# Eighteen feed-forward up pairs of a decoder layer in Strassen's form, with the down projection as a phase of its own

## The chip, the core and the metric

The kernel runs on one core of a Trainium2 chip (trn2). The metric is device time in microseconds, the median of several executions; one further execution is taken by the hardware profiler, and all rows below are from it. The engines are TensorE (PE, with its weight loads as PEld), VectorE (DVE), ScalarE (ACT), GpSimd (POOL) and the queue engine SyncE (SP), which issues most of the DMAs.

## The reference, cut to what matters

One decoder layer for 1,024 prompt tokens and 8 x 4 sample tokens, T = 1,056 tokens in all, in float32. The change lies in the last third of the layer, the feed-forward:

```
h2 = rmsnorm(x, w['norm2_g'])
up = h2 @ w['ffn_up']                      # 1024 -> 2 * 2816
up_ext = concatenate([ffn_hist, up])       # 2 tokens of history
g_ff, u_ff = split(causal_dwconv(up_ext, w['ffn_conv_w'], w['ffn_conv_b']))   # 3 taps
x = x + (silu(g_ff) * u_ff) @ w['ffn_down']                                   # 2816 -> 1024
```

A final RMSNorm follows, and the last two rows of `up_ext` are an output too.

## The kernel before

Data lie channels first: 128 channels on the partitions, the 1,056 tokens along the free axis, cut into three chunks of 352 columns (CH). A product in nearly full float32 precision is made of three matmuls in the fp32r format: each operand is split into an upper part (cast to fp32r) and a lower part (the remainder), and hi x hi, hi x lo and lo x hi are summed in PSUM. `product` (line 1968) does one block of 128 output channels so: 8 k-blocks x 3 parts x 3 chunks = 72 matmuls of 352 columns, each with its own weight load. The input projections, the gates, the output projection and the up projection all use it.

The feed-forward works on 22 pairs of blocks, a gate block and an up block of 128 channels each. Per block: SP loads 128 weight columns (512 KB) into a ring of three buffers, GpSimd casts and subtracts (`split`, lines 884 to 888), TensorE runs `product` into ps0 or ps1 (three PSUM banks each), DVE evicts with the norm factor (`ffn_tokens`), ACT does the first tap of the convolution (line 1345), DVE the other two (line 1894), ACT the silu (1348), DVE the product (1900), ACT and DVE split the result into act_hi and act_lo (1355, 1906). The down projection of each two pairs (24 sets of 6 matmuls of 352 columns, `down`, lines 2518 to 2541) stands in TensorE's program between two up blocks of later pairs; its sets alternate between the two banks pt0 and pt1, and DVE adds each into the residual x1 = y_all in SBUF (`ffn_sums`, line 1914). A loop turn on every engine is two pairs. The order of the instructions is written out by hand, engine by engine, with semaphores. A helper, `Order.run`, makes an engine wait for its own last result before it goes on.

Ahead of it stands the output projection (`out_block`), whose result is x1; `second_norm_upper` and `second_norm_lower` make h = x1 * norm gain in two parts, and the row factor rstd (a square root on ACT, a reciprocal on DVE) is applied at eviction. At the end, TensorE turns the history rows (`turn_ffn_state`, 44 transposes) and the result (`turn_tile`), ACT and DVE normalize, and SP stores. `TAIL` and `TAIL_DVE` give the order of the last sums and tiles.

Of the kernel before, what the change touches and what calls it, by code (L numbers as in the profile page):

```python
# [29 lines left out]
P = 128  # L30
# [18 lines left out]
FH = 2  # L49
EPS = 1e-6  # L50
# [69 lines left out]
class Order:  # L120
# [31 lines left out]
    def enter(self, i, first, extra=()):  # L152


        per = {name: n - self.before.get(name, 0) for name, n in self.n.items()}
# [11 lines left out]
def decoder_layer(nc, a, o):  # L167
# [15 lines left out]
    h_hi = sb(top, "h_hi", [P, KD, T], F32R)  # L183
    h_lo = sb(top, "h_lo", [P, KD, T], F32R)
    y_all = sb(top, "y_all", [P, 2 * 4, T])
    w_raw = [sb(top, f"w_raw{n}", [P, KD, P]) for n in range(2)]
    w_hi = [sb(top, f"w_hi{n}", [P, KD, P], F32R) for n in range(2)]
    w_lo = [sb(top, f"w_lo{n}", [P, KD, P], F32R) for n in range(2)]
# [158 lines left out]
    ld_pw, ld_ws = sem("ld_pw"), sem("ld_ws")  # L347
# [4 lines left out]
    w_zeroed, small_zeroed, a_zeroed = sem("w_zeroed"), sem("small_zeroed"), sem("a_zeroed")  # L352
# [9 lines left out]
    dk_abs, dk_exp, dk_u, dk_ln = sem("dk_abs"), sem("dk_exp"), sem("dk_u"), sem("dk_ln")  # L362
    alog_exp, sdt_done = sem("alog_exp"), sem("sdt_done")
    a_sum, a_rms, va_done, u_done = sem("a_sum"), sem("a_rms"), sem("va_done"), sem("u_done")
    wst_done, wsm_done, pd_done = sem("wst_done"), sem("wsm_done"), sem("pd_done")
    pstate_in, pstate_out, y_a_done = sem("pstate_in"), sem("pstate_out"), sem("y_a_done")
# [30 lines left out]
    def ptf_of(b):  # L397
# [52 lines left out]
    att_zeroed, att_rows, v_done = sem("att_zeroed"), sem("att_rows"), sem("v_done")  # L450
# [3 lines left out]
    c_zeroed, sx_ready, clog_in, clog_done = sem("c_zeroed"), sem("sx_ready"), sem("clog_in"), sem("clog_done")  # L454
    ld_pages, ld_lf, ld_v = sem("ld_pages"), sem("ld_lf"), sem("ld_v")
    ld_k = [sem(f"ld_k{n}") for n in range(2)]
    ss_max, ss_exp, ss_done = sem("ss_max"), sem("ss_exp"), sem("ss_done")
    x_conv, x_act, xstate_in, xst_ready, z_done = (sem(n) for n in ("x_conv", "x_act", "xstate_in", "xst_ready",
                                                                    "z_done"))
    d_zeroed, ld_d, eacs_done = sem("d_zeroed"), sem("ld_d"), sem("eacs_done")  # L460
# [5 lines left out]
    d_rms, yd_ready = sem("d_rms"), sem("yd_ready")  # L466
# [14 lines left out]
    s46 = ExitStack()  # L481
    hist_f = sb(s46, "hist_f", [9 * FH, 2 * FF])
    fh = sb(s46, "fh", [P, 2 * NFF, NB * FH])
    fstate = sb(s46, "fstate", [P, 2 * NFF, 9 * FH])
    f_raw = w_raw + [sb(s46, "w_raw2", [P, KD, P])]
    f_hi = w_hi + [sb(s46, "w_hi2", [P, KD, P], F32R)]
    f_lo = w_lo + [sb(s46, "w_lo2", [P, KD, P], F32R)]
# [5 lines left out]
    ones_m = sb(s4, "ones_m", [P, P])  # L493
    s4.close()
    ext = [sb(s46, f"ext{n}", [P, FE_W + 4]) for n in range(2)]
    cv = [sb(s46, f"cv{n}", [P, FE_W]) for n in range(2)]
    act_hi = sb(s46, "act_hi", [P, 2, T], F32R)
    act_lo = sb(s46, "act_lo", [P, 2, T], F32R)
    s46.close()

    y_out = [f_raw[n][:, :, :].rearrange("p k n -> p (k n)") for n in range(3)]
    gfin = ext[1][:, 0:D]
# [11 lines left out]
    ones_done, nm_full, nm_rms, h2_hi_done, h2_split = (sem(n) for n in ("ones_done", "nm_full", "nm_rms",  # L514
# [2105 lines left out]
```

## Time and profile before

| | |
|---|---|
| runs | 1920.19, 1922.92 and 1929.63 us, median 1922.92 |
| the profiled execution | 1923.46 us, of which the trace spans 1921.7 us |
| mean granted TensorE clock | 0.986 |
| TensorE busy | 96% of the span, 11,458 matmuls |
| VectorE, GpSimd, ScalarE busy | 47%, 30%, 21% |
| DMA | 113.51 MB, mean 59 GB/s |

The feed-forward lasts from about 1114 us to the end. Matmuls overlap in the trace: a matmul's recorded duration is longer than the distance to the next one's start, and rates are read from the starts.

### The profile page before, as it was taken

How to read it: one execution, taken by the hardware profiler on the slowest of the kernel's cores; microseconds unless marked ns; L12 is line 12 of the kernel's file. 1: busy time of each engine (PE TensorE's matmuls, PEld its weight loads, DVE VectorE, ACT ScalarE, POOL GpSimd, SP SyncE). 2: the span in 40 equal slices, each digit the busy share in tenths (PEclk: the TensorE clock that was granted, in tenths of full speed). 3: DMA queues.
4: the chain of work that ended last, by engine and by line, in shares of the span. 5: the costliest groups of instructions: out<-in, count | busy, mean ns of one | idle time of the engine just before them, and what ended most of it. 6: DMA issues, size and time to landing. Idle time of an engine off the chain costs nothing.

```text
span 1921.7 us, 29631 instructions
## 1 busy us (share of the span) xinstructions
PE 1849.8 (96%) x11458; PEld 1776.4 (92%) x11458; DVE 908.9 (47%) x1390; ACT 404.2 (21%) x583; POOL 582.9 (30%) x532
## 2 busy tenths in 40 slices
PE   5899999999999998999999999999999999999997
PEld 4889978888899978999999999999999999999986
DVE  5763244326533434222253375555555555555555
ACT  5210033423311112110121131111111111211123
POOL 2223310022233323334342324423432432432420
PEclk9899999999999989999999999999999999999998
DMA  4121130022122222232224311111111111211102
GB/s 126 46 53 38 46 90 23 12 83 67 39 86 68 69 73 73 62 94 72 68 77 108 100 34 55 45 35 54 55 33 44 55 44 33 64 45 33 55 11 99
DMA packets 156104, 113.51 MB, mean 59 GB/s; under 512 B 10743, under 2 KB 146652, under 8 KB 155991
## 3 DMA queue, kind: packets, MB, share of 16 engines
q1 hardware_dynamic: 153084, 102.61, 19.1%
q10 hardware_dynamic: 2940, 9.81, 1.3%
q8 instruction: 55, 0.90, 0.2%
q14 instruction: 25, 0.20, 0.0%
HBM read 95.37 MB, written 16.99 MB: 58 GB/s over the span
## 4 chain that ended last, share of the span: by engine, by line
PE 90%; DVE 5%; ACT 2%; DMA 1%; issue 1%; POOL 0%; ACTq 0%; SPq 0%; DVEq 0%; POOLq 0%
PE ps L1976 21%; PE ps L1982 20%; PE ps L1979 20%; PE ps L2413 5%; PE pt L2538 4%; PE pt L2540 4%; PE pt L2539 4%; PE ps L2185 2%; PE ps L2146 2%; PE pt L2171 1%; PE ps L2538 1%; PE ps L2540 1%; PE ps L2539 0%; PE ps L2118 0%; PE ps L2292 0%
## 5 line engine op out<-in xcount | busy, mean ns | idle before, releaser
L1976 PE MATMUL ps<-h_hi,w_hi 128*128 128x352 f32 x2472 | 549.6, 331 | 10.4 <-POOL w_lo L888 4.5
L1982 PE MATMUL ps<-h_hi,w_lo 128*128 128x352 f32 x2472 | 534.9, 324 | 0.0
L1979 PE MATMUL ps<-h_lo,w_hi 128*128 128x352 f32 x2472 | 534.5, 324 | 0.0
L1976 PEld LDWEIGHTS ps<-h_hi,w_hi 128*128 128x128 f32 x2472 | 417.5, 190 | 22.0 <-issue 13.6
L1982 PEld LDWEIGHTS ps<-h_hi,w_lo 128*128 128x128 f32 x2472 | 425.2, 189 | 0.0
L1979 PEld LDWEIGHTS ps<-h_lo,w_hi 128*128 128x128 f32 x2472 | 422.8, 189 | 0.0
L881 POOL TENSOR_TENSOR mark<-eps 128x1 f32<-128x1 f32 x159 | 52.2, 329 | 1080.4 <-PE ps L1982 558.0
L888 POOL TENSOR_TENSOR w_lo<-w_raw,w_hi 128x1024 fp32r<-128x1024 f32 x127 | 332.9, 2621 | 10.2
L1914 DVE TENSOR_TENSOR y_all<-y_all,pt 128x352 f32<-128x352 f32 x234 | 122.0, 522 | 104.7 <-PE pt L2540 104.5
L2538 PE MATMUL pt<-act_hi,w_hi 128*128 128x352 f32 x468 | 152.9, 327 | 3.7 <-DVE y_all L1914 2.2
L2540 PE MATMUL pt<-act_hi,w_lo 128*128 128x352 f32 x468 | 152.4, 326 | 0.0
L2539 PE MATMUL pt<-act_lo,w_hi 128*128 128x352 f32 x468 | 152.0, 325 | 0.0
L1894 DVE SCALAR_TENSOR_TENSOR cv<-ext,pv,cv 128x1072 f32<-128x1072 f32 x88 | 144.7, 1645 | 11.9 <-DVE cv L1894 0.2
L887 POOL CAST w_hi<-w_raw 128x1024 fp32r<-128x1024 f32 x127 | 133.0, 1047 | 0.0
L1345 ACT ACTIVATE cv<-ext,pv 128x1072 f32<-128x1072 f32 x44 | 56.6, 1287 | 305.0 <-DVE ext L1883 305.0
L1880 DVE TENSOR_TENSOR ext<-ps,cst 128x704 f32<-128x704 f32 x44 | 39.3, 893 | 123.4 <-PE ps L1982 123.0
L2538 PEld LDWEIGHTS pt<-act_hi,w_hi 128*128 128x128 f32 x468 | 88.9, 190 | 4.9 <-DVE y_all L1914 2.9
L1355 ACT ACTIVATE act_hi<-cv 128x1024 fp32r<-128x1024 f32 (+1 forms) x44 | 28.4, 646 | 302.7 <-DVE cv L1900 302.0
L2539 PEld LDWEIGHTS pt<-act_lo,w_hi 128*128 128x128 f32 x468 | 89.0, 190 | 0.0
L2540 PEld LDWEIGHTS pt<-act_hi,w_lo 128*128 128x128 f32 x468 | 88.8, 190 | 0.0
L1269 ACT ACTIVATE sg<-ps 128x1056 f32<-128x1056 f32 x16 | 16.9, 1053 | 214.2 <-PE ps L1982 214.2
L1809 DVE TENSOR_TENSOR sg<-sg,ps 128x1056 f32<-128x1056 f32 x8 | 10.0, 1254 | 85.8 <-PE ps L2413 85.7
(346 smaller groups left out, 1882.1 us busy)
## 6 DMA issues: line engine op xcount, KB each, us to landing
w_raw<-in_w_in SPq DMA_DIRECT2D x52, 512.0 KB, 4.4
w_raw<-in_ffn_up SPq DMA_DIRECT2D x44, 512.0 KB, 3.8
w_raw<-in_ffn_down SPq DMA_DIRECT2D x22, 512.0 KB, 3.5
gates_dram<-y_all ACTq DMA_DIRECT2D x16, 528.0 KB, 2.7
cst<-gates_dram SPq DMA_DIRECT2D x16, 528.0 KB, 3.6
x_tok<-in_x_prompt SPq DMA_DIRECT2D x8, 512.0 KB, 4.1
bw_raw<-in_w_branch SPq DMA_DIRECT2D x32, 128.0 KB, 3.5
w_raw<-in_w_out SPq DMA_DIRECT2D x8, 512.0 KB, 5.1
```

What stands on the lines that cost most here:

```text
L887: od.run(g.tensor_copy(hi, raw))
L888: od.run(g.tensor_tensor(lo, raw, hi.bitcast(F32), ALU.subtract), w_split)
L1345: od.run(sc.activation(cv[k][:, 0:FE_W - FH], x[:, 0:FE_W - FH], ACT.Identity, scale=param(PV_FW, blk), bias=param(PV_FB, blk)), cv0_done)
L1894: od.run(v.scalar_tensor_tensor(cv[k][:, 0:w], x[:, j:j + w], pv[:, bass.ds(blk + (PV_FW + 2 * NFF * j), 1)], cv[k][:, 0:w], ALU.mult, ALU ...
L1914: od.run(v.tensor_tensor(dst, dst, spare_or_pt(n, spare), ALU.add), dn_done)
L1976: mm(dst[:, c, 0:CH], f_hi[n][:, k, :], h_hi[:, k, tok], start=k == 0, stop=False)
L1979: mm(dst[:, c, 0:CH], f_hi[n][:, k, :], h_lo[:, k, tok], start=False, stop=False)
L1982: last = mm(dst[:, c, 0:CH], f_lo[n][:, k, :], h_hi[:, k, tok], start=False, stop=k == KD - 1)
L2413: last = mm(dst[:, c, 0:CH], w[q % 2][:, k, :], y[:, 2 * q + k, c * CH:(c + 1) * CH], start=k == 0 and n == 0, stop=k == 1 and n == 2)
L2538: mm(dst, w[:, m, :], act_hi[:, k, tok], start=k == 0, stop=False)
L2539: mm(dst, w[:, m, :], act_lo[:, k, tok], start=False, stop=False)
L2540: last = mm(dst, w_rest[:, m, :], act_hi[:, k, tok], start=False, stop=k == 1)
```

## The change

The first four pairs (NPL = 4) stay plain products with a ring of two weight buffers. The other 18 pairs (NST) are done in the Winograd form of Strassen's scheme. For a pair the left matrix has two rows, the gate block and the up block, and two columns, the halves of the 1,024 input channels; the right matrix, h, is cut into halves of channels and halves of 528 tokens. Seven half products (4 k-blocks x 3 parts x 2 chunks of 264 columns, 168 matmuls) replace the eight of a plain pair. For this

- the norm factors are multiplied into x1 once (`normalize_x1`), the four combinations of the right side (h quarters T1 to T4) are made and split once, by DVE and ACT, in the space of h_hi, h_lo and y_all; before that x1 is stored to DRAM (`save_x1`) and it comes back later (`x_acc`);
- GpSimd makes four combinations of the weights of every pair and seven remainders, ACT the seven upper casts;
- the seven half products go into three accumulators, X (ps0), Y (ps1) and Z (pt0, pt1), and ACT and DVE take partial sums out between them (`left_save`, `part_out`, `second_half_out`, `first_half_out`) into buffers from which the halves of the gate and up blocks arise;
- the activations of each pair are stored to DRAM (`store_act`) and loaded again for the down projection, which is one phase behind all up pairs: 11 groups of two blocks, four PSUM banks in turn. The history rows are turned within its second group.

Semaphores are merged and renumbered elsewhere without a change of order. The core of the diff:

```diff
+NPL = 4
+NST = NFF - NPL
+TH = T // 2
+CC = TH // 2
+KH = KD // 2
...
+    RIGHT = [h_op(Q_B11), sum_op(OP_T2), h_op(Q_B21), h_op(Q_T3), sum_op(OP_T1), sum_op(OP_T4), h_op(Q_B22)]
+    INTO = [(x_dst, True), (y_dst, True), (x_dst, False), (y_dst, False), (z_dst, True), (y_dst, False), (z_dst, False)]
```

TensorE, the seven half products of a pair:

```diff
+        def strassen(q):
+            first = isinstance(q[0], int) and pair_of(q) == 0
+            for n, (dst, start) in enumerate(INTO):
+                pe.wait_ge(a_split, of(q, 7, n + 1))
+                if first:
+                    if n in (0, 2, 3, 6):
+                        pe.wait_ge(right_split, {0: 4, 2: 5, 3: 7, 6: 6}[n])
+                    else:
+                        pe.wait_ge(right_split, {1: 2, 4: 1, 5: 3}[n])
+                if first and n < 2:
+                    pe.wait_ge(up_read, 2 * NPL - 1 + n)
+                elif n in (0, 2):
+                    pe.wait_ge(x_read, of(q, 2, n // 2))
+                elif not (first and n == 4):
+                    pe.wait_ge(u_read, of(q, 5, {1: -1, 3: 1, 4: 0, 5: 2, 6: 3}[n]))
+                hi, lo = slots[n][:, 0, :, :], slots[n][:, 1, :, :]
+                right_hi, right_lo = RIGHT[n]
+                for k in range(KH):
+                    for c in range(2):
+                        mm(dst(c), hi[:, k, :], right_hi[:, k, c * CC:(c + 1) * CC], start=start and k == 0, stop=False,
+                           skip_group_check=True)
+                    for c in range(2):
+                        mm(dst(c), hi[:, k, :], right_lo[:, k, c * CC:(c + 1) * CC], start=False, stop=False,
+                           skip_group_check=True)
+                    for c in range(2):
+                        last = mm(dst(c), lo[:, k, :], right_hi[:, k, c * CC:(c + 1) * CC], start=False, stop=k == KH - 1,
+                                  skip_group_check=True)
+                last.then_inc(p_full, 1)
```

GpSimd, the weights of a pair (`slot_unused` waits in the first pair for the last plain product and for right_split 7, else for the same half product of the pair before):

```diff
+        def split_pair(q, raw):
+            gp.wait_ge(ld_s[raw], q[0] * 32 + 32)
+            od.run(g.tensor_tensor(s1, a21, a22, ALU.add), s_added)
+            od.run(g.tensor_tensor(s2, s1, a11, ALU.subtract), s_added)
+            remainder(q, 0, a11)
+            remainder(q, 1, s2)
+            remainder(q, 2, a12)
+            slot_unused(q, 3)
+            od.run(g.tensor_tensor(s3, a11, a21, ALU.subtract), s_added)
+            remainder(q, 3, s3)
+            remainder(q, 4, s1)
+            remainder(q, 5, a22)
+            slot_unused(q, 6)
+            od.run(g.tensor_tensor(s4, a12, s2, ALU.subtract), s_added)
+            remainder(q, 6, s4)
```

ScalarE, from the last plain pair on:

```diff
+        plain_tap(3, 0)
+        gate_silu(3, 7)
+        cast((0, 0), 0, 0)
+        cast((0, 0), 0, 1)
+        for q in range(4):
+            quarter_upper(q)
+        for n in range(2, 7):
+            cast((0, 0), 0, n)
...
+        def st_pair(q, nxt=None):
+            left_save(q)
+            if nxt is not None:
+                cast(nxt, (s + 1) % 2, 0)
+            if first:
+                plain_tap(NPL - 1, 1)
+            else:
+                first_tap(pair_of(q, NPL - 1), 0, None, (u_read, of(q, 5, 0)),
+                          of(q, 2, 2 * NPL - 3 if isinstance(i, int) and pair_of(q) == 1 else 2 * NPL - 2))
+            if nxt is not None:
+                cast(nxt, (s + 1) % 2, 1)
+            if not first:
+                gate_silu(None, of(q, 2, 2 * NPL))
+            first_half_out(q, 2 * NPL if first else of(q, 2, 2 * NPL))
+            if nxt is not None:
+                for n in range(2, 6):
+                    cast(nxt, (s + 1) % 2, n)
+            else:
+                act_upper(0, 0)
+            first_tap(e, 1, None, (u_read, of(q, 5, 4)), of(q, 2, 2 * NPL if first else 2 * NPL - 1))
+            if nxt is not None:
+                cast(nxt, (s + 1) % 2, 6)
```

VectorE, a pair in the loop:

```diff
+            else:
+                second_half_out((i, s - 1), 6, 0, u2)
+                later_tap(pair_of(q, NPL - 1), 0, of(q, 2, 2 * NPL), (1,))
+                dve.wait_ge(x_read, of(q, 2, 1))
+                part_out(q, 1, by_bank(u2), by_bank(e1))
+                later_tap(pair_of(q, NPL - 1), 0, None, (2,))
+                ffn_product(pair_of(q, NPL))
+            part_out(q, 3, by_bank(u3), by_bank(e1))
+            second_half_out(q, 4, 1, u3)
+            part_out(q, 5, by_bank(ext[1][:, FH:FH + TH]), by_bank(e1))
+            later_tap(e, 1, of(q, 2, 2 * NPL + 1))
```

VectorE, the plain pairs and the step to the first Strassen pair:

```diff
+        ffn_tokens(0, 0)
+        normalize_x1()
+        later_tap(0, 0, 1)
+        ffn_tokens(0, 1)
+        od.run(v.tensor_tensor(raw_sum(OP_T1), x_part(0, 1), x_part(0, 0), ALU.subtract), t_added)
...
+        ffn_tokens(3, 0)
+        later_tap(3, 0, 7)
+        for q in range(3):
+            quarter_lower(q)
+        ffn_tokens(3, 1)
+        quarter_lower(Q_T3)
```

SP, the step to the down phase, and the order of the tail:

```diff
+        load_down(0, 0)
+        load_act(0, 0)
+        load_act(0, 1)
+        sp.wait_ge(x1_sent, 16 * KD)
+        sp.wait_ge(p_full, 7 * (NST - 1) + 2)
+        sp.dma_start(x_acc[:, 0:KH, :], x_saved[:, 0:KH, :]).then_inc(ld_x1[0], 16)
+        store_act(NFF - 2)
+        sp.wait_ge(p_full, 7 * (NST - 1) + 5)
+        sp.dma_start(x_acc[:, KH:KD, :], x_saved[:, KH:KD, :]).then_inc(ld_x1[1], 16)
...
-    TAIL = [("sums", 0, 16), ("state", 4), ("tile", 0), ("tile", 1),
-            ("sums", 16, 20), ("tile", 2), ("sums", 20, 24)] + [("tile", t) for t in range(3, NT + 1)]
+    TAIL = [("sums", 0, 16), ("sums", 16, 18), ("tile", 0), ("tile", 1),
+            ("sums", 18, 20), ("tile", 2), ("sums", 20, 24)] + [("tile", t) for t in range(3, NT + 1)]
```

## Rows read from the trace of the kernel before

**Rows 1.** The page, busy time and share of each engine:
```profile
PE 1849.8 (96%) x11458; PEld 1776.4 (92%) x11458; DVE 908.9 (47%) x1390; ACT 404.2 (21%) x583; POOL 582.9 (30%) x532
```
**Rows 2.** Busy time by stretch: stretch, length, engines, clock, DMA share, GB/s:
```profile
1152.26:1813.48 661.22, 661.22 (x4105) 661.22 (x4105) 361.83 (x509) 104.34 (x135) 233.97 (x174) 1.00 0.16 46
```
**Rows 3.** The chain of waits in order of time (start, length, what):
```profile
1152.26 0.49 PE ps L1982 x3
...
1813.48 0.49 PE ps L1982 x3
```
**Rows 4.** Timeline of TensorE in an up product (start, length, instructions):
```profile
1502.03 0.64 PE L1976 MATMUL ps<-h_hi,w_hi 128*128 128x352 f32 x3
...
1504.91 0.64 PE L1976 MATMUL ps<-h_hi,w_hi 128*128 128x352 f32 x3
```
**Rows 5.** Busy time by stretch, the start of the last down group:
```profile
1871.08:1874.20 3.12, 3.12 (x11) 3.12 (x12) 0.52 (x1) 1.43 (x3) 0.00 (x0) 0.53 0.02 5
```
**Rows 6.** Timeline of TensorE in the tail:
```profile
1860.11 1.48 PE L2565 MATMUL ps<-cst,fstate 128*18 128x128 f32 x12
...
1871.08 0.66 PE L2538 MATMUL pt<-act_hi,w_hi 128*128 128x352 f32 x1 [1.43 <-DVE act_lo L1906]
1871.55 0.49 PE L2539 MATMUL pt<-act_lo,w_hi 128*128 128x352 f32 x1
...
1873.60 0.49 PE L2540 MATMUL pt<-act_hi,w_lo 128*128 128x352 f32 x1
...
1888.20 2.03 PE L2576 MATMUL ps<-cst,y_all 128*128 128x128 f32 x16
...
1894.39 0.59 PE L2538 MATMUL pt<-act_hi,w_hi 128*128 128x352 f32 x1 [2.23 <-DVE y_all L1914]
```
**Rows 7.** Timeline of TensorE, short matmuls of the scan:
```profile
563.30 1.00 PE L2308 MATMUL ps<-xdt,seg 128*128 128x64 f32 x8
564.14 0.66 PE L2325 MATMUL ps<-xte,xb 128*128 128x128 f32 x4
```
**Rows 8.** Instructions of VectorE by line and shape (count, busy us, mean ns, idle before):
```profile
L1894 DVE SCALAR_TENSOR_TENSOR cv<-ext,pv,cv 128x1072 f32<-128x1072 f32 x88 | 144.7, 1645 | 11.9 <-DVE cv L1894 0.2 <-DVE fstate L1892 0.2
L1914 DVE TENSOR_TENSOR y_all<-y_all,pt 128x352 f32<-128x352 f32 x234 | 122.0, 522 | 104.7 <-PE pt L2540 104.5
L1880 DVE TENSOR_TENSOR ext<-ps,cst 128x704 f32<-128x704 f32 x44 | 39.3, 893 | 123.4 <-PE ps L1982 123.0
L1906 DVE TENSOR_TENSOR act_lo<-cv,act_hi 128x1024 fp32r<-128x1024 f32 x22 | 27.6, 1253 | 33.1 <-ACT act_hi L1355 33.1
L1873 DVE RECIPROCAL cst<-cst 128x1056 f32<-128x1056 f32 x1 | 6.8, 6753 | 5.2 <-ACT cst L1326 5.2
```
**Rows 9.** Timeline of VectorE, two taps with GpSimd idle and busy:
```profile
1145.72 2.71 DVE L1894 SCALAR_TENSOR_TENSOR cv<-ext,pv,cv 128x1072 f32<-128x1072 f32 x2
...
1156.18 3.68 DVE L1894 SCALAR_TENSOR_TENSOR cv<-ext,pv,cv 128x1072 f32<-128x1072 f32 x2
```
**Rows 10.** Instructions of ScalarE by line and shape:
```profile
L1345 ACT ACTIVATE cv<-ext,pv 128x1072 f32<-128x1072 f32 x44 | 56.6, 1287 | 305.0 <-DVE ext L1883 305.0
L1348 ACT ACTIVATE cv<-cv 128x1072 f32<-128x1072 f32 x22 | 24.2, 1102 | 0.7
L1157 ACT ACTIVATE pr_t<-pt 128x512 f32<-128x512 f32 x24 | 14.4, 600 | 1.6 <-PE pt L2171 0.9
L1298 ACT ACTIVATE y_all<-ps 128x1056 f32<-128x1056 f32 x8 | 8.4, 1056 | 76.5 <-PE ps L2469 76.5
L1340 ACT ACTIVATE ext<-fh 128x16 f32 x36 | 8.0, 221 | 8.2 <-ACT act_hi L1355 4.6
```
**Rows 11.** Instructions of GpSimd by line and shape:
```profile
L888 POOL TENSOR_TENSOR w_lo<-w_raw,w_hi 128x1024 fp32r<-128x1024 f32 x127 | 332.9, 2621 | 10.2
...
L962 POOL TENSOR_TENSOR bw_lo<-bw_raw,bw_hi 128x256 fp32r<-128x256 f32 x32 | 25.4, 794 | 2.6
```
**Rows 12.** Busy time by stretch, the first loads:
```profile
0.00:10.00 10.00, 0.00 (x0) 0.00 (x0) 0.06 (x1) 2.90 (x4) 3.09 (x8) 1.00 0.85 267
```

More of the change, by code:

```diff
@@ L150, in peel, with enter @@
         self.before = dict(self.n)
[L152 to L155 removed]
+    def enter(self, i, first, extra=(), times=1):
+        per = {name: (n - self.before.get(name, 0)) * times for name, n in self.n.items()}
         per.update({s.name: k for s, k in extra})
@@ L1044, in _ @@
+        od.peel()
+        for s in range(2):
+            split_down(0, s)
+        with gp.Fori(1, N_DOWN // 2) as i:
+            od.enter(i, 1)
+            for s in range(2):
+                split_down(i, s)
+        od.leave(N_DOWN // 2 - 1)
+        split_down(N_DOWN // 2, 0)
     @block.scalar
@@ new lines, in cast @@
+        def cast(q, raw, n):
+            first = isinstance(q[0], int) and pair_of(q) == 0
+            gate, up = pair_raw[raw]
+            src = (gate[:, 0:KH, :], s_tmp[1][:, :, :], gate[:, KH:KD, :], s3_tmp[:, :, :],
+                   s_tmp[0][:, :, :], up[:, KH:KD, :], s6_tmp[:, :, :])[n]
+            if first and n == 0:
+                act.wait_ge(up_full, 2 * NPL - 1)
+            elif first and n == 2:
+                act.wait_ge(up_full, 2 * NPL)
+            elif first and n == 4:
+                act.wait_ge(right_split, 7)
+            elif not first:
+                act.wait_ge(p_full, of(q, 7, n + 1 - 7))
+            if n in (0, 2, 5):
+                act.wait_ge(ld_s[raw], q[0] * 32 + 32)
+            else:
+                act.wait_ge(s_added, of(q, 4, {1: 2, 3: 3, 4: 1, 6: 4}[n]))
+            od.run(sc.activation(slots[n][:, 0, :, :], src, ACT.Copy), s_cast)
@@ new lines, in act_upper @@
+        def act_upper(i, s):
+            act.wait_ge(ld_a[s], i * 16 + 16)
+            if isinstance(i, int) and i == 0:
+                act.wait_ge(p_full, 7 * (NST - 1) + 3 + s)
+            else:
+                act.wait_ge(dn_full, i * 48 + (24 * s - 24))
+            od.run(sc.activation(act_hi[s], act_raw[s], ACT.Copy), act_hi_done)
+        st_pair((0, 0), (0, 1))
+        od.peel()
+        st_pair((0, 1), (1, 0))
+        with act.Fori(1, NST // 2 - 1) as i:
+            od.enter(i, 1, times=2)
+            st_pair((i, 0), (i, 1))
+            st_pair((i, 1), (i + 1, 0))
@@ L1941, in _ @@
-        od.leave(NFF // 2 - 1)
+        st_pair((0, 1))
+        with dve.Fori(1, NST // 2 - 1) as i:
+            od.enter(i, 1, times=2)
+            for s in range(2):
+                st_pair((i, s))
+        od.leave(NST // 2 - 2)
+        st_pair((NST // 2 - 1, 0))
+        st_pair((NST // 2 - 1, 1), lambda: act_lower(0, 0))
+        second_half_out((NST // 2 - 1, 1), 6, 0, u2)
+        dve.wait_ge(ld_x1[0], 16)
+        dve.wait_ge(ld_x1[1], 16)
+        ffn_sums(0, 0, down_sets(), 0, 2)
@@ L2485, in _ @@
         out_block(1, 1)
-        with pe.Fori(2, KD // 2 - 1) as i:
-            for s in range(2):
-                out_block(i, s)
+        for s in range(2):
+            out_block(2, s)
         out_block(KD // 2 - 1, 0)
@@ L2569, in turn_tile @@
+            lo, hi = STATES[n]
+            for b in range(lo, hi):
+                last = tr(flat(0)[0:9 * FH, (b - lo) * P:(b - lo + 1) * P], fstate[:, b, :], ident)
+            last.then_inc(st_full, 1)
+        down(0, 0)
+        down(0, 1, between={4 + 5 * n: [lambda n=n: turn_ffn_state(n)] for n in range(len(STATES))})
+        with pe.Fori(1, N_DOWN // 2) as i:
+            for s in range(2):
+                down(i, s)
         def turn_tile(t):
             r = rows_of(t)
-            n = len(STATES) + t
```

844 lines of the change are left out of this document (524 added, 320 removed).

## The prediction

> **What bounds the kernel now.** I read the page's busy times first: TensorE is busy for 96% of the span, the others for 47% at most [rows 1]. The table by stretch says the same of the stage that changes: from 1152 to 1813 us TensorE has no idle time at all, VectorE is busy for 55% and GpSimd for 35% [rows 2]. So the feed-forward goes as fast as TensorE's matmuls follow each other, and the next question is how fast that is. The chain of waits in order of time gives it over the whole loop: the same point of the loop's body is passed at 1152.26 and, 9.5 turns later, at 1813.48 [rows 3]. A turn is 69.6 us; it issues four up products of 72 matmuls and 24 down sums of 6, 432 in all, so one matmul costs 161.1 ns. The timeline shows the same undisturbed: 18 matmuls from 1502.03 to 1504.91, 160.0 ns each [rows 4]. The durations of about 0.32 us in the lists are not costs, for matmuls overlap; only the distance of starts is one.
>
> **The price of a matmul of 264 columns.** This decides the case, and no row shows it. 352 columns at 2.4 GHz are 146.7 ns, so 13.3 ns of the 160.0 are something else. At a granted clock of 0.53, that is the 1.2 GHz level [rows 5], seven matmuls take 2.05 us, 293 ns each [rows 6], and 352 columns at 1.2 GHz are 293.3: nothing else is left there. Weight loads are hidden in both cases. If the 13.3 is a fixed part, 264 columns cost 110.0 + 13.3 = 123.3 ns, and with the loop's 161.1 to 160.0, 124.2. If it grows with the columns, it is 161.1 x 0.75 = 120.8. The other end: the period is held by the loading of 128 weight columns and doesn't shrink, 161.1. The nearest row for that is a stream of 64 moving columns, each with its own 128 weight columns: 8 in 0.84 us, 105 ns [rows 7]. A weight load alone thus needs no more than 105 ns, and 264 columns still cover it. I take 124.2, the fixed part, and keep 110 and 161 as ends.
>
> The Trainium skill ("TensorE: Matmul & The Clock Gate", Back-to-back issue gap) gives a matmul alone N / 2.4 + 2.5 ns at the full clock. For N = 352 that is 149.2, and the trace has 160.0, so it doesn't hold for these operands here; by it the new matmul would cost 112.5 ns and the sum below would be 35 us lower.
>
> **Removed and added on TensorE.** An up pair is now 144 matmuls, 144 x 0.1611 = 23.20 us. The new pair is seven half products of 4 k-blocks x 3 parts x 2 column halves = 168 matmuls, 168 x 0.1242 = 20.87 us. One eighth of the columns goes (50,688 to 44,352), but one sixth more matmuls pay the fixed part. That is 2.33 us a pair, **-42 us** for 18 pairs. The 11 down groups keep their 144 matmuls each, and four pairs stay as they are.
>
> **Does the pair's chain keep up?** A half product takes 24 x 0.1242 = 2.98 us, and the tightest wait is that of the fourth one (onto the second accumulator), which needs DVE's first partial sum; it starts 5.96 us after the first one ends. In between stand, in order: the drain of the last matmul (0.32 us long at 0.16 spacing: 0.16); ACT's copy of 528 columns out of PSUM, 0.62, and a cast of 512, 0.60 (600 ns at 512); a small copy, 0.22; the first tap of the former pair's gate, 1.29 [rows 10]; on DVE the history copy, about 0.2, one tap of 1.36 us, and a sum of 528 columns, 0.71 (522 at 352 and 893 at 704 give 1.05 ns a column) [rows 8, 9]. That is 5.2 us; seven handovers add some 0.6, an estimate. 5.8 against 5.96 just fits. While GpSimd subtracts, two taps take 3.68 instead of 2.71 us [rows 9], so one may be 0.5 longer: I charge 0.1 us a pair, **+2 us**. All of DVE's work in a pair is about 12.3 us (four taps, three sums of 528, two second halves of 1.0, a product of 1.5), 15 with contention. GpSimd has eleven operations on 512 columns: between 794 ns at 256 and 2,621 at 1,024 lies 1.40 [rows 11], 15.4 us of 20.9. Neither is the bound, but the cover is thin: at one microsecond of stall a pair the 18 pairs lose 18 us.
>
> **The four plain pairs.** Their products take 11.6 us each, and DVE must free a PSUM buffer in time. At the start it does the reciprocal (6.75 us [rows 8]), one eviction (1.7: 0.89 for 704 columns, two smaller ones behind it), and then, newly, eight scalings of the residual ahead of the taps. As 1,056-column operations of three operands like the taps these are 8 x 1.45 = 11.6 us, then 3.2 for two taps and 1.7 for the next eviction: 25 to 26 us, when the fourth product could have started at 23.2. The operand sums (2,112 columns, twice the 1,056 class of about 1.25 [rows 8]: 2.4 us each) come in the same queue, but by the third pair DVE has caught up. **+3 us.**
>
> **The first Strassen pair.** Here the order on ACT costs. Counted from the start of the last plain product (E, its end, is at 11.6): eviction of the gate 2.1, ACT's tap 3.45, DVE's taps 6.6, silu 7.8, two casts 9.1, then the upper copies of four quarters of h, 1.95 each (1.06 at 1,056 columns [rows 10]), to 17.1. DVE subtracts behind each, 2.35 (1.25 at 1,024 [rows 8]), the first done at 13.6: the first half product starts 2.1 us late. The second needs PSUM that DVE frees only behind the third subtraction, at 20.1: 3.5 us more. The third waits until ACT has copied the first one out, and that copy stands in ACT's program behind five casts, the last of which wants GpSimd's fourth combination. GpSimd waits with its third for the fourth quarter's remainder (22.5), then does two combinations and three remainders of 1.4 with casts between, to 30.2; cast and copy end at 31.5. The second product ended at 23.2: 8.3 us more. In all 13.9 us without matmuls. After idle times of 1.4 and 2.2 us the timeline shows TensorE at half pace for some 2.8 and 3.3 us [rows 6], so each of the two long stops also costs about 1.5: **+17 us.**
>
> **Into the down phase.** DVE's first sums need x1 back from DRAM. Behind the last pair's second product 1.08 MB of activations twice, 4.3 MB of x1 and a 0.54 MB store want the queue, 7 MB; at the 267 GB/s of the first 10 us [rows 12] that is 26 us from 2.9 us on, some 8 us after the last half product. Four PSUM banks let TensorE run 3.9 us ahead: **+4 us.** Afterwards a group's 24 sums of 522 ns [rows 8] and the subtraction stay under its 23.2 us.
>
> **The tail.** Before, TensorE goes from 1860.11 to 1871.08 with 42 transposes and waits for the last activations, and then runs at half pace for ten matmuls [rows 5, 6]. The transposes (about 4.7 us) move among down sums and the rest, 11.0 + 1.3 - 4.7 = 7.6, goes. Against it two sums now stand ahead of the first output tile; its transposes start 1.9 us later and with them the restart that comes 6.2 us after them (1888.20 to 1894.39 [rows 6]). **-5.5 us.**
>
> **Sum.** -42 + 2 + 3 + 17 + 4 - 5.5 = -21.5: span 1921.7 to 1900.2. The profiled execution took 1923.46, 1.8 outside its span and 0.5 above the median of 1922.92, so I forecast **1901 us**.
>
> **Rivals.**
> *The chain inside a pair doesn't fit.* DVE's and GpSimd's contention, or handovers of 0.2 us, make it late by 0.8 to 1.6 us a pair: 1901 + 12 to 27 = 1913 to 1928. For it speaks the margin of 0.16 us; against it that only operations with both operands in SBUF stretch. Chance 0.20.
> *The matmul doesn't shrink enough (the other side).* Place: the 168 matmuls; price: 3.02 us for each ns above 124.2. From 131 ns on the change is a loss. At 140, the straight line from the short matmuls to the 352, it ends at 1949; at 161 at 2012. Against it stands the row of 105 ns [rows 7]. The skill's LDWEIGHTS section of the same page says that the time goes by weight columns alone, so a shorter stream covers less of it; the row agrees. Chance 0.14.
> *The first pair's and the down phase's stalls are smaller, or the extra part grows with the columns.* 120.8 ns saves 10 us more, half the stalls 12: 1879 to 1891. Chance 0.12.
> *The matmul costs N / 2.4 and 2.5 ns.* 1866, if the 13.3 belongs to the 352 alone. By the skill's gap rule above; the row at 352 speaks against it. Chance 0.04.
>
> **Numbers.** My forecast, with its own range of 1888 to 1913, has 0.50. Of a measurement of this kernel 0.5% (9.6 us) can be told from no change. Faster by that (under 1913): 0.50 + 0.16 and nearly nothing of the first rival, 0.65; within 0.5% (to 1932): 0.20; slower 0.15. The range that leaves about a tenth outside at each end is 1876 to 1934.
>
> **What would show it.** Starts of 264-column matmuls 124 ns apart in an undisturbed stretch; turns of the new loop (two pairs) of 42 us; TensorE's waits for ACT's copy and DVE's sums in the first Strassen pair, some 14 us; a wait for the x1 load at the start of the down phase; no wait ahead of the last down group. Matmuls 130 ns or more apart, or a wait in every pair on DVE's first partial sum, would make it wrong.

## The result and the profile after

The changed kernel takes 1954.2 us (median of four runs, 1950.4 to 1956.5) against 1923.9 for the kernel before on the same chip: ratio 1.0153, 95% interval 1.0122 to 1.0184. The forecast was 1901. The profiled execution took 1953.35 us with a span of 1951.5, 29.8 above the span of before; forecast were 21.5 below.

The busy times of the page, the busy time by stretch (the whole Strassen stage; the first 3.24 us behind one wait; an undisturbed piece), and TensorE's waits from 1000 us on (engine, line, released by: us in total, times, longest):

```profile
PE 1825.3 (94%) x11890; PEld 1746.5 (89%) x11890; DVE 989.5 (51%) x1463; ACT 511.8 (26%) x716; POOL 724.1 (37%) x622
```

```profile
1220.92:1659.20 438.28, 395.44 (x3024) 391.12 (x3025) 253.48 (x310) 178.86 (x253) 292.82 (x200) 0.94 0.25 80
...
1404.22:1407.46 3.24, 3.24 (x14) 3.24 (x15) 1.99 (x2) 1.62 (x2) 0.15 (x1) 0.50 0.00 0
1407.75:1426.01 18.26, 18.26 (x153) 18.26 (x152) 8.73 (x14) 7.61 (x12) 13.60 (x10) 1.00 0.26 80
```

```profile
PE ps L2956 <- DVE y_all L2274: 33.8, 18, 2.5
PE ps L2956 <- ACT y_all L1634: 8.2, 1, 8.2
PE ps L2956 <- issue: 6.0, 1, 6.0
...
PE ps L2399 <- DVE ext L2199: 4.5, 2, 3.3
PE pt L2983 <- DVE x_acc L2324: 4.3, 1, 4.3
PE ps L2983 <- DVE x_acc L2324: 2.2, 2, 1.5
PE pt L2983 <- DVE ext L2284: 1.2, 1, 1.2
PE ps L2956 <- DVE ext L2199: 0.9, 1, 0.9
```

Where [rows 2] showed a stage without any idle time, TensorE now waits for VectorE's partial sums (y_all, line 2274). Fourteen of the 18 pairs wait 2.0 to 2.2 us ahead of the fourth half product, for the first partial sum. Of the others, the first pair does not wait for it, two pairs wait 0.5 us, and the last pair waits 0.3 us there and 2.5 us ahead of its sixth half product, for the second sum. The timeline of TensorE around two of the long waits:

```profile
1401.67 0.40 PE L2962 MATMUL ps<-hq_hi,w_hi 128*128 128x264 f32 x2
1404.22 0.81 PE L2956 MATMUL ps<-hq_hi,w_lo 128*128 128x264 f32 x2 [2.14 <-DVE y_all L2274]
1404.82 0.64 PE L2959 MATMUL ps<-hq_lo,w_lo 128*128 128x264 f32 x2
1405.26 0.64 PE L2962 MATMUL ps<-hq_hi,w_lo 128*128 128x264 f32 x2
...
1411.65 0.41 PE L2956 MATMUL ps<-t_op,slot 128*128 128x264 f32 x2
...
1414.57 0.41 PE L2956 MATMUL pt<-hq_hi,slot 128*128 128x264 f32 x2
...
1428.58 0.51 PE L2956 MATMUL ps<-hq_hi,w_lo 128*128 128x264 f32 x2 [2.17 <-DVE y_all L2274]
```

Two things are to be seen. The matmuls are a little cheaper than forecast: 24 from 1411.65 to 1414.57 are 121.7 ns each. And a wait of 2.1 us can cost more than itself: behind the first one two matmuls take 0.44 us, 220 ns each, which is 264 columns at 1.2 GHz (the granted clock of that stretch is 0.50), for some 3 us; behind the second the pace is full. Such a fall comes in 9 of the 14 pairs; they last 24.4 us (1404.22 to 1428.58), the other five 22.9.

What TensorE waits for is read from the chain of waits in order of time:

```profile
1414.77 0.64 ACT slot L1606
1416.16 1.29 ACT cv L1567
1417.92 2.31 DVE cv L2211
1420.36 2.15 DVE cv L2211
1422.90 0.44 DVE ext L2282
1423.37 0.41 DVE ext L2283
1424.31 1.29 ACT cv L1567
1426.10 1.52 DVE cv L2211
1427.81 0.72 DVE y_all L2274
1428.58 0.51 PE ps L2956 x2
```

It doesn't begin at the new pair's first half product, as the forecast had it. It begins at the end of the former pair's sixth (1414.6): ScalarE's cast and tap of the up half, VectorE's two up taps, the second half that VectorE writes into the gate's buffer, and only then the gate's first taps and the sum. That is 14.0 us, against four half products, 11.8 us. (Behind the last pair's 2.5 us stands something else: VectorE's product, stretched beside GpSimd, ahead of the second sum.)

### The profile page after: what moved, and what is told of

Its sections match the earlier page's. It is cut to its first block, busy times and chain, and to the rows that moved or that the text cites. A ratio compares the mean times of both kernels' runs of the same rounds, so it can differ in the third digit from the quotient of the medians.

```text
span 1951.5 us, 31730 instructions
## 1 busy us (share of the span) xinstructions
PE 1825.3 (94%) x11890; PEld 1746.5 (89%) x11890; DVE 989.5 (51%) x1463; ACT 511.8 (26%) x716; POOL 724.1 (37%) x622
## 4 chain that ended last, share of the span: by engine, by line
PE 71%; DVE 19%; ACT 5%; issue 2%; DMA 1%; ACTq 1%; POOL 1%; DVEq 0%; SPq 0%; POOLq 0%
PE ps L2399 12%; PE ps L2405 11%; PE ps L2402 11%; DVE cv L2211 6%; PE ps L2836 4%; PE ps L2956 2%; ACT cv L1567 2%; PE ps L2959 2%; PE ps L2962 2%; PE pt L2983 2%; PE pt L2985 2%; PE pt L2984 2%; PE ps L2983 2%; PE ps L2608 2%; PE ps L2984 2%
## 5 line engine op out<-in xcount | busy, mean ns | idle before, releaser
L2399 PE MATMUL ps<-h_hi,w_hi 128*128 128x352 f32 x1608 | 363.5, 334 | 14.2 <-POOL w_lo L1062 5.2
L2405 PE MATMUL ps<-h_hi,w_lo 128*128 128x352 f32 x1608 | 349.6, 325 | 0.0
L2402 PE MATMUL ps<-h_lo,w_hi 128*128 128x352 f32 x1608 | 348.9, 325 | 0.0
L2399 PEld LDWEIGHTS ps<-h_hi,w_hi 128*128 128x128 f32 x1608 | 270.9, 191 | 26.2 <-issue 16.9
L2405 PEld LDWEIGHTS ps<-h_hi,w_lo 128*128 128x128 f32 x1608 | 278.0, 190 | 0.0
L2402 PEld LDWEIGHTS ps<-h_lo,w_hi 128*128 128x128 f32 x1608 | 276.1, 190 | 0.0
L1062 POOL TENSOR_TENSOR w_lo<-w_raw,w_hi 128x1024 fp32r<-128x1024 f32 x69 | 177.1, 2567 | 5.5
L2324 DVE TENSOR_TENSOR x_acc<-x_acc,pt 128x352 f32<-128x352 f32 x136 | 70.9, 521 | 51.1 <-PE pt L2985 48.3
L2324 DVE TENSOR_TENSOR x_acc<-x_acc,ps 128x352 f32<-128x352 f32 x128 | 66.7, 521 | 41.8 <-PE ps L2985 37.9
L2956 PE MATMUL ps<-hq_hi,w_hi 128*128 128x264 f32 x288 | 60.6, 293 | 14.2 <-ACT y_all L1634 8.2
L2962 PE MATMUL ps<-hq_hi,w_hi 128*128 128x264 f32 x288 | 60.4, 292 | 0.0
```

The lines of the kernel that those rows point to most:

```text
L1062: od.run(g.tensor_tensor(lo, raw, hi.bitcast(F32), ALU.subtract), w_split)
L2324: od.run(v.tensor_tensor(dst, dst, sum_bank(n, last), ALU.add), dn_done)
L2399: mm(dst[:, c, 0:CH], f_hi[n][:, k, :], h_hi[:, k, tok], start=k == 0, stop=False)
L2402: mm(dst[:, c, 0:CH], f_hi[n][:, k, :], h_lo[:, k, tok], start=False, stop=False)
L2405: last = mm(dst[:, c, 0:CH], f_lo[n][:, k, :], h_hi[:, k, tok], start=False, stop=k == KD - 1)
L2956: mm(dst(c), hi[:, k, :], right_hi[:, k, c * CC:(c + 1) * CC], start=start and k == 0, stop=False, skip_group_check=True)
```

## The experiments

Executions of one kernel lie up to 0.9% apart (1916 to 1933 us for the kernel before), and the first half product starts anywhere between 1216 and 1228 us where nothing ahead of it was edited. So below the length of the Strassen stage (first to last half product, in the profiled execution; 438.3 us in the changed kernel) is compared beside the median. Ratios are to the kernel before.

**The first sum ahead of the gate's later taps.**

```diff
-                later_tap(pair_of(q, NPL - 1), 0, of(q, 2, 2 * NPL), (1,))
                 dve.wait_ge(x_read, of(q, 2, 1))
                 part_out(q, 1, by_bank(u2), by_bank(e1))
-                later_tap(pair_of(q, NPL - 1), 0, None, (2,))
+                later_tap(pair_of(q, NPL - 1), 0, of(q, 2, 2 * NPL))
```

> Only VectorE's order in a pair is changed: the sum that frees the second accumulator (first partial sum) stands ahead of the gate's two later taps, not between them. Theory A (order: the wait of the fourth half product hangs on VectorE's queue, which holds the former pair's up taps of 4.6 us, its second half, and ScalarE's and VectorE's first gate taps, 14.0 us from the end of the sixth half product where TensorE has 11.8 us of work): about 4 us leave that chain, so the 18 waits of 33.8 us in all vanish, and with them some 20 us at half pace behind them: 1954 - 54 = about 1900, 1895 to 1912. Theory B (engines too full: VectorE is late anyway, and the delayed second and third sums become the next wait): waits of 1 us or more a pair move to the sixth or seventh half product, 1925 to 1945. Theory C (the operands' remainders on GpSimd set the pace): no change, 1950 to 1957.

Measured: 1916.2 us, ratio 0.9969 (0.9952 to 0.9986), stage 402.0. No wait for the fourth half product is left, and from the second pair to the last but one none runs at half pace. A smaller wait, 12.6 us in all, has moved to the sixth, onto the second sum; 2.6 us of it, with half pace behind, are the last pair's. TensorE's and VectorE's timeline (one pair):

```profile
1419.12 0.51 PE L2955 MATMUL ps<-t_op,slot 128*128 128x264 f32 x2 [0.74 <-DVE y_all L2274]
```

```profile
1412.01 3.61 DVE L2211 SCALAR_TENSOR_TENSOR cv<-ext,pv,cv 128x1072 f32<-128x1072 f32 x2 [0.15 <-DVE fstate L2209]
1416.79 1.22 DVE L2218 TENSOR_TENSOR cv<-cv 128x1024 f32<-128x1024 f32 x1 [1.17 <-ACT cv L1572]
1418.05 0.19 DVE L2219 TENSOR_TENSOR act_n<-cv 128x32 f32<-128x32 f32 x1
1418.36 0.71 DVE L2274 TENSOR_TENSOR y_all<-ps,y_all 128x528 f32<-128x528 f32 x1
```

The second sum stands behind two taps of 3.61 us (2.7 without GpSimd), a wait of 1.17 us for silu, and the product. So theory A holds for the cause, and the total was 4 us worse than its range because the next wait in VectorE's queue was at hand, at the place that theory B named.

**The second half ahead of the second up tap, alone.** The first sum stays between the gate's taps.

```diff
-            later_tap(e, 1, of(q, 2, 2 * NPL + 1))
+            later_tap(e, 1, of(q, 2, 2 * NPL + 1), (1,))
...
                 second_half_out((i, s - 1), 6, 0, u2)
+                later_tap(pair_of(q, NPL - 1), 1, None, (2,))
...
```

> Against the changed kernel one edit: the former pair's second half goes out between the two up taps; the first partial sum stays between the gate's taps. It asks which chain holds the fourth half product. Theory A (only the queue in front: what my prediction left out is that VectorE comes to the second half behind two stretched up taps): one tap of 2.3 us leaves the chain of 14.0 us, 11.7 is left against TensorE's 11.8, the waits of 33.8 us go: 1903 to 1912. Theory B (the chain that my prediction put at 5.8 us, from the end of the first half product over ScalarE's copy, cast and tap to VectorE's tap and sum, is itself too long): in the run with both moved it took some 8.1 us to the end of the gate's first later tap and a sum of 0.7, against 5.9 us of cover; the wait stays at 2 us a pair: 1946 to 1956.

Measured: 1922.9 us, ratio 1.0001 (0.9984 to 1.0019), stage 404.1; the waits of the fourth half product shrink to 0.5 to 1.1 us in nearly all pairs (14.1 in all), and from the second pair on half pace is gone. The time lies between the two theories' ranges. Neither theory is right alone: the queue in front gave about half of the wait, and when it is shorter the chain that the prediction did count holds the rest. Its timeline on ScalarE, VectorE and TensorE:

```profile
1525.96 0.61 ACT L1634 ACTIVATE y_all<-ps 128x528 f32<-128x528 f32 x1 [0.88 <-PE ps L2964]
1526.78 0.63 ACT L1606 ACTIVATE w_hi<-w_raw 128x512 fp32r<-128x512 f32 x1 [0.21 <-ACT y_all L1634]
...
1528.10 1.28 ACT L1567 ACTIVATE cv<-ext,pv 128x1072 f32<-128x1072 f32 x1 [0.33 <-ACT ext L1559]
...
1529.84 2.05 DVE L2211 SCALAR_TENSOR_TENSOR cv<-ext,pv,cv 128x1072 f32<-128x1072 f32 x1
1532.10 0.71 DVE L2274 TENSOR_TENSOR y_all<-ps,y_all 128x528 f32<-128x528 f32 x1 [0.21 <-DVE cv L2211]
1532.87 0.51 PE L2958 MATMUL ps<-hq_hi,w_lo 128*128 128x264 f32 x2 [1.07 <-DVE y_all L2274]
```

From ScalarE's copy at 1525.96 to TensorE at 1532.87 are 6.9 us, where the prediction had 5.6 (its 5.8 less the drain): the tap takes 2.05 us instead of 1.36, and the gaps between these instructions add up to 1.23 us instead of 0.6.

**Both edits.**

> As the run with the sum first, and besides the former pair's second half goes out between the two up taps, not behind them. Theory A: if the first edit leaves no wait in the pairs, this one moves nothing that anybody waits for: the same time within 0.3%, about 1900. If the first edit leaves a wait on the second partial sum (it ends 0.2 us or less before TensorE needs it by my working), this one gives 2 us of room and removes it, some 3 to 10 us. Theory B: still waits of 1 us a pair, 1925 to 1945.

Measured: 1925.9 us, ratio 1.0013 (0.9996 to 1.0031), stage 408.4, 6 us longer than with the first edit alone. The waits of the sixth half product grew from some 0.7 us to some 1.1, since the earlier second half lets other instructions of VectorE and GpSimd meet: the gate's two taps took 1.84 and 2.13 us here, where the first edit alone had 1.34 and 2.13. The expectation's working, which counted on 2 us of room, was wrong; waits of 1 us a pair and a time in its range are what theory B had forecast.

**GpSimd's work made small, order unchanged.** Part of the weights is stale.

```diff
+            if not isinstance(q[0], int):
+                lo, src, hi = (x[:, 0:1, 0:64] for x in (lo, src, hi))
             od.run(g.tensor_tensor(lo, src, hi.bitcast(F32), ALU.subtract), a_split)
...
```

The four combinations and two of ScalarE's casts are made small in the same way.

> The order stays as it is; in the loop's pairs GpSimd's eleven operations work on 64 of 512 columns, and so do ScalarE's two casts of the sums that are built in place, so part of the weights is stale. It asks how much of the wait comes from VectorE's taps being stretched while GpSimd runs. Contention: two up taps take 2.7 us, not 4.6, and the gate's tap 1.35, not 1.5: the chain of 14.0 us becomes 12.0 against TensorE's 11.8, so the wait shrinks from 2.0 to some 0.2 us a pair and the half pace goes: 1900 to 1912. Handovers and order alone: the taps keep 4.6 us or the wait stays over 1.5 us a pair, 1940 to 1955.

Measured: 1912.9 us, ratio 0.995 (0.9933 to 0.9968), stage 395.1. VectorE's taps by line and shape over the pairs (count, busy us, mean ns), first the changed kernel, then this one:

```profile
L2211 DVE SCALAR_TENSOR_TENSOR cv<-ext,pv,cv 128x1072 f32<-128x1072 f32 x65 | 120.9, 1860 | 8.5 <-DVE fstate L2209 1.7 <-DVE y_all L2274 0.2
```

```profile
L2220 DVE SCALAR_TENSOR_TENSOR cv<-ext,pv,cv 128x1072 f32<-128x1072 f32 x65 | 86.9, 1337 | 8.5 <-DVE fstate L2218 2.1 <-DVE y_all L2283 0.2
```

A tap falls from 1.86 to 1.34 us; VectorE's sums from PSUM keep their 708 ns in both. The three taps on the path of 14.0 us take 4.0 us together instead of 6.0, the wait shrinks to 0.35 to 0.44 us a pair, and half pace is gone behind the first pair: with unstretched taps the change's own order nearly fits. What is left is the path that the prediction did count; from ScalarE's copy on it takes 6.2 us here, not 5.6. Contention was expected to carry this, and does, though the time is 0.9 us above the range given.

**The second sum ahead of the product as well.**

```diff
-                ffn_product(pair_of(q, NPL))
             part_out(q, 3, by_bank(u3), by_bank(e1))
+            ffn_product(NPL if first else pair_of(q, NPL))
...
```

> As the run with the first sum ahead of the gate's taps (1916, where 16 waits of the sixth half product on the second partial sum, 12.6 us in all, were left), and the second partial sum ahead of the product too. Theory: it then waits for the gate's taps alone, not for silu (1.1 us) and the product (1.5 us), and is ready about 1.9 us before TensorE needs it: the 12.6 us go, 1916 - 12 = 1904 (1900 to 1909). Rival (VectorE and ScalarE are full, the later product delays the store and the next pair's taps): the waits come back elsewhere, 1912 to 1920.

Measured: 1919.7 us, ratio 0.999 (0.9972 to 1.0007), stage 402.2: no gain, as the rival had it. All waits for VectorE's sums are gone, but every second pair now waits for ScalarE's copy, and the last pair 3.9 us. Timeline of GpSimd, ScalarE and TensorE:

```profile
1530.34 2.26 POOL L1223 TENSOR_TENSOR s_tmp<-w_raw,s_tmp 128x512 f32<-128x512 f32 x1
1532.63 0.63 ACT L1606 ACTIVATE slot<-s_tmp 128x512 fp32r<-128x512 f32 x1 [3.00 <-POOL s_tmp L1223]
1533.79 0.61 ACT L1634 ACTIVATE y_all<-ps 128x528 f32<-128x528 f32 x1 [0.53 <-ACT slot L1606]
1534.45 0.51 PE L2954 MATMUL ps<-hq_hi,w_hi 128*128 128x264 f32 x2 [1.29 <-ACT y_all L1634]
```

The copy stands behind the seventh cast, which waits for GpSimd's fourth combination, stretched to 2.26 us by VectorE's taps.

**The first pair.** ScalarE's copy of the first accumulator is moved ahead of its last four casts; a second run moves the last plain pair's tap too (the line with plain_tap is the second's alone).

```diff
-        for n in range(2, 7):
-            cast((0, 0), 0, n)
...
+                cast(q, 0, 2)
+                act.wait_ge(right_split, 6)
+                left_save(q)
+                plain_tap(NPL - 1, 1)
+                for n in range(3, 7):
+                    cast(q, 0, n)
```

> Only the first Strassen pair: ScalarE copies its first accumulator out behind the third cast and three of the four subtractions of h's quarters, not behind all seven casts. Order theory: the third half product's wait of 8.2 us goes and with it 2.6 us at half pace: 1954 - 10.8 = about 1943 (1941 to 1946). Rival: the operands of the third and fourth products come late anyway (GpSimd's third combination waits for the last quarter): half of the 8.2 us comes back at the fourth product, about 1949. The waits of the other 17 pairs stay.

> Against the changed kernel, the first Strassen pair alone: as in the run that copied the first accumulator out early, where the 8.2 us came back as 9.1 us at the sixth half product, and ScalarE's tap of the last plain pair's up half is issued ahead of the fourth to seventh cast too. Theory (the stall is one of ScalarE's order: VectorE's second sum stands behind the taps that wait for that tap): neither wait is left over 2 us, and 2.6 us at half pace go: 1954 - 10 = 1944 (1941 to 1948). Rival (the operands come late: GpSimd's third combination waits for the last quarter of h, its fourth stands behind three remainders): a wait of 4 us or more on the operands shows, 1949 to 1957.

Measured: 1959.0 us, ratio 1.0182 (1.0155 to 1.021), stage 439.7; and 1959.1, ratio 1.0174 (1.0135 to 1.0212), stage 438.1. No gain, and both times lie above either range: the 8.2 us came back, in the first run at the sixth half product and in the second in the next pair (TensorE's timeline of each run):

```profile
1252.96 0.56 PE L2960 MATMUL ps<-t_op,slot 128*128 128x264 f32 x1 [9.06 <-DVE y_all L2278]
```

```profile
1261.91 0.78 PE L2959 MATMUL ps<-hq_hi,w_hi 128*128 128x264 f32 x2 [6.50 <-ACT y_all L1631]
```

Each edit took away the place of the stall, not its source. It was shown that the order of the copy is not the source. That GpSimd's late start on the first pair is the source is borne out in part by the last two runs below, which differ only in the first pair's edits: with ScalarE's order much as in the second run here and GpSimd's third combination let go earlier, 4.3 us are left in the second pair, not 6.5, where ScalarE's copy stands behind a cast of GpSimd's fourth combination. The stage is only 2.4 us shorter by it.

**The loads ahead of the down phase, and the scalings.** The second pair of activations is loaded behind x1, and the eight scalings of the residual stand behind the second eviction.

> Two edits in two other stages of the changed kernel, each read from its own wait. At the start of the plain pairs the eight scalings of the residual stand behind the second eviction: the wait of 3.3 us for it goes; if VectorE is then late for the next, it comes back at the fifth product. Ahead of the down phase the second pair of activations is loaded behind both halves of x1, not ahead of them: 1.08 MB less in front, at some 270 GB/s 4.0 us, so the first down sums' waits of 7.7 us shrink to 3 or 4. Both together: 1954 - 7 = 1947 (1944 to 1950). Rival (the loads are held by their waits for TensorE, not by the queue; VectorE is late for the fifth product): 1951 to 1957.

Measured: 1957.2 us, ratio 1.0164 (1.013 to 1.0198), no gain. The wait of 3.3 us became one of 5.7 at a later product, and the first half product came 7.3 instead of 6.0 us late. The waits at the start of the down phase stayed (1.6, 1.6 and 0.7 us). The expectation had read the tail's 4.3 us into them by mistake.

**Everything that a trace pointed to.** Besides both sums first: ScalarE's third cast of the next pair ahead of silu; in the last pair the up taps behind TensorE's first down sums. The combined run adds the first pair's edits (GpSimd's third combination no longer waits for the last quarter) and four scalings moved.

```diff
                 cast(nxt, (s + 1) % 2, 1)
+                cast(nxt, (s + 1) % 2, 2)
...
-                for n in range(2, 6):
+                for n in range(3, 6):
```

> Every order edit that a trace pointed to, together, and no computation left out: both partial sums ahead of what waits for silu; ScalarE's third cast of the next pair ahead of silu (with the sums first, every second pair still waited 1.2 us for the first accumulator's copy, which stood behind GpSimd's fourth combination, and GpSimd had waited for that cast); in the last pair the activations' remainders and the up taps behind the sums that TensorE waits for; in the first pair GpSimd's third combination no longer waits for the last quarter of h, and ScalarE's fourth cast, copy and tap are issued ahead of the other casts; four of the eight scalings of the residual behind the second eviction. Theory (all the lost time is order, none of it an engine that is full): the Strassen stage, 438 us in the changed kernel and 402 with the sums first, comes near 3024 matmuls of 0.122 us and a start at half pace, 372 to 382; the plain pairs' wait of 3.3 goes: 1920 - 25 - 3 = about 1892 (1884 to 1900), faster than before by 1.5%. Rival (GpSimd with 16 to 18 us of work a pair and its handovers is the bound at 21.3 us a pair): the stage stays at 390 or more, 1905 to 1915.

> As the combined run, without its edits to the first pair and to the scalings: the 8.2 us and the half pace of the first pair stay. Theory: the stage is 386 to 392 us, the whole 1905 (1898 to 1910). Rival (GpSimd bounds the pairs): 398 or more, 1914 to 1920.

Measured: combined 1911.4 us, ratio 0.994 (0.9921 to 0.9959), stage 386.8; pairs only 1913.0, ratio 0.9939 (0.9917 to 0.9962), stage 389.9. In the second the same point of the loop, two pairs apart, and VectorE's first down sum:

```profile
1449.78 0.52 PE L2960 MATMUL ps<-hq_hi,w_hi 128*128 128x264 f32 x2 [0.21 <-ACT y_all L1634]
...
1491.80 0.52 PE L2960 MATMUL ps<-hq_hi,w_hi 128*128 128x264 f32 x2 [0.19 <-ACT y_all L1634]
1617.57 1.08 DVE L2324 TENSOR_TENSOR x_acc<-x_acc,ps 128x352 f32<-128x352 f32 x2 [3.68 <-DMA x_acc<-x_dram]
```

A turn is 42.02 us, the forecast's 42; without its waits of 0.4, 123.8 ns a matmul. So GpSimd isn't the bound at 21.3 us a pair. With the pairs' edits only, the stage was where theory put it (386 to 392) and the whole 8 us worse than its 1905: what follows the stage took 6.3 us more than in the changed kernel, as the down phase began with waits of 6.2 us, not 3.4. With the up taps out of the way, VectorE waited 3.7 us for x1. The combined run missed both: its stage lies above the theory's 372 to 382, with a wait of 4.2 us left in the second pair, and its time is 19 us above the forecast, in the rival's range though not by the rival's reason.

**The load again, and the first pair with it.**

> As the run with the pairs' order alone (1913), and the second pair of activations loaded behind both halves of x1. In the changed kernel that edit moved nothing, because VectorE's up taps and second half stood ahead of the first sums anyway; with them moved away the first sums waited 3.7 us for the load of x1, and the down phase began with waits of 6.2 us. Theory (now the load is on the path): 1.08 MB less in front at about 420 GB/s is 2.6 us, so the wait falls to 1 or 2 us: 1910 (1905 to 1914). Rival (the load is held by the release of x1's place, not by the queue): no change, 1911 to 1916.

> The same with the first pair's edits of the combined run (but the scalings of the residual left where they were, since behind the eviction they cost more than they gave). In the combined run the first pair's stage was only 3 us shorter, as a wait of 4.2 us came back in the second pair on ScalarE's copy. If those 3 us add up with the load: 1907 (1902 to 1911), 0.8% faster than before. Rival (the gain of the first pair is in the spread of the runs): the same as the run with the load alone, within 0.15%.

Measured: 1913.0, ratio 0.9943 (0.9925 to 0.9961), and 1912.9, ratio 0.994 (0.9917 to 0.9963): no further gain, and no difference between the two, as the second's rival had it. VectorE's wait for x1 stayed 3.7 us, so the load isn't held by the activations in front of it. The first run's timeline of SP, VectorE and TensorE shows what stood in front:

```profile
1603.45 0.36 SPq L949 DMA_DIRECT2D act_dram<-cv  x1
...
1604.33 0.79 SPq L1013 DMA_DIRECT2D x_acc<-x_dram  x1
...
1612.74 1.08 DVE L2324 TENSOR_TENSOR x_acc<-x_acc,ps 128x352 f32<-128x352 f32 x2 [3.73 <-DMA x_acc<-x_dram]
...
1600.21 0.41 PE L2960 MATMUL ps<-t_op,slot 128*128 128x264 f32 x2
```

The second half of x1 needs the place that the fifth half product frees. That one was over at 1600.4 (the sixth begins at 1600.21), but SP issues the load only at 1604.33, right behind the store of the last pair but one, and this store waits for VectorE's product (done at 1603.4). So it is SP's order that holds the load; a run with the load ahead of that store wasn't made. The order edits together make the change 0.6% faster than the kernel before, and that is what is left of it.

## Why the prediction was wrong

The terms, from the last transposes of the stage ahead (which end 1.3 us earlier than before, so the stages behind it lost 31.1 us):

| term | forecast, us | measured, us |
|---|---|---|
| matmuls of 18 pairs | -42 | -43.2 (168 at 123.8 ns against 23.20 us) |
| chain inside a pair | +2 | +49.9 (33.8 of waits, 16.1 of half pace; 5.5 of both are the last pair's) |
| plain pairs and first Strassen pair | +20 | +24.5 (4.5, then 6.0 + 0.9 + 8.2, and 4.9 of half pace) |
| into the down phase | +4 | +3.4 (1.2 + 2.2) |
| tail | -5.5 | -3.5 (what is left, all else included) |

Half pace is worked out: the stage of 438.3 us less 3024 matmuls at 123.8 ns (374.4) and waits of 42.9 leaves 21.0; of that the first and third half products of the first pair, at 5.6 and 5.2 us instead of 2.97, take 4.9. The last row is a remainder and no measurement of the tail: it also holds some 1.6 us at half pace behind the wait of 3.3 us in the plain pairs, and a wait of 1.2 us of the kernel before, at the start of its second up product, that is gone.

**The step that failed is "Does the pair's chain keep up?"**, which let 5.8 us just fit into 5.96 and charged 0.1 us a pair. It failed in three ways. First, it let VectorE be free when ScalarE's tap is done. But that tap waits for the second half, and the second half stands behind the former pair's two up taps; this path, 14.0 us against 11.8, wasn't counted at all. Second, the path that it did count takes 7.1 us, not 5.8 (6.9 from ScalarE's copy on; 1525.76 to 1532.87 in the run with the second half early). The margin of 0.16 us could not carry a stretched tap: the prediction allowed 0.5 us for one tap, and three stand on the longer path. Third, it priced a stall at its own length, although the paragraph on the first pair, from [rows 6], adds half pace to a long stop. The first rival named the place but gave it 0.8 to 1.6 us a pair; in 14 pairs it was 2.1 of waiting, and half pace came to 0.9 a pair on average.

The runs show that the order and the contention were both needed for the stall: taking away either one (the sum moved ahead, or GpSimd made light) takes away most of it.

**What was right.** The price of the matmul within some 2%; that neither VectorE nor GpSimd is the bound; the first pair's stall of 8.3 us behind the casts, measured 8.2. Whether the extra time of a matmul is a fixed part stays open: undisturbed it should have made 123.3 ns, a part that grows with the columns 120.0, and 121.7 lies between.

**What agreed by luck.** The first pair lost 15.1 us in waits against 13.9, but its start was late by 6.0 us instead of 2.1 and its second product by 0.9 instead of 3.5. The late start has the failed step's cause once more. VectorE came to the gate's eviction 3.5 us after the last plain product began (1203.10), behind the former pair's up taps and product; ScalarE's tap had its input at 1208.28 and then waited 1.3 us more for the store of that pair's activations (VectorE's and ScalarE's timeline):

```profile
1206.64 0.89 DVE L2196 TENSOR_TENSOR ext<-ps,cst 128x704 f32<-128x704 f32 x1
...
1209.55 1.28 ACT L1567 ACTIVATE cv<-ext,pv 128x1072 f32<-128x1072 f32 x1 [6.25 <-DMA act_dram<-act_n]
```

The down phase's 3.4 us agree in size only: VectorE's queue held it, and the x1 load, which the prediction blamed, had landed 3.3 us before VectorE came to its first sum.

**Readings that were off without changing the outcome.** The 1.4 us stop in [rows 6] did not bring half pace by itself: the granted clock was 0.50 from 1867.2 us on, behind a stop of 2.8 us. In [rows 7] the first start is 60 ns from the second and the others lie 111 ns apart, which 264 columns cover as well. The second rival's straight line gives 143 ns at 264 columns, not 140.

## What to carry to other kernels

A wait is as long as the longest path to it, and that path runs through whatever stands ahead in the waiting engine's queue, back into the former turn of the loop; write VectorE's queue out for two turns before trusting a margin. With a margin of 3% of a path, price every operation on it at its contended duration. After an edit of order, look for the next wait at once: here four runs (the second sum, both of the first pair, the scalings) only moved a stall.

## What the runs showed of the hardware

VectorE's taps and GpSimd's subtractions wait for each other rather than slow down. In the changed kernel a tap starts at 1417.92 while GpSimd runs from 1417.80 to 1419.09, and takes 2.31 us instead of 1.34; GpSimd's next operation, at 1421.44, starts during the second tap (to 1422.51) and takes 2.21 instead of 1.29. Each is longer by about what the other had left. VectorE's sums, which read one operand from PSUM, keep 708 ns beside GpSimd's full work and beside the light one. The Trainium skill ("SBUF — State Buffer", Who interferes with whom) says that an operation of VectorE with two inputs in SBUF and one of GpSimd that reads SBUF exclude each other for a whole instruction; the trace agrees. Even a short operation pays: in the product that the changed kernel does during the last pair, 32 columns that elsewhere take 0.19 us took 2.23, to the end of GpSimd's subtraction (timeline of both):

```profile
1646.43 3.21 POOL L1248 TENSOR_TENSOR w_lo<-w_raw,w_hi 128x1024 fp32r<-128x1024 f32 x1
1647.46 2.23 DVE L2219 TENSOR_TENSOR act_n<-cv 128x32 f32<-128x32 f32 x1
```

Waits of up to 1.3 us, one or two in each pair, left TensorE's granted clock at 1.00 in the runs that had them (the first sum ahead, both edits, the second sum). Waits of 2.0 to 2.2 us, one in each pair, brought it to 0.50, which is 1.2 GHz, in 9 of 14 pairs of the changed kernel, some 3 us each time; a single wait of 2.0 us in the run with the second half early did not.
